# Delta rule: the transposes of three block-diagonal matrices on VectorE in 32x32 blocks, instead of on TensorE as products with the identity

## What is computed

```python
def gated_delta_chunked(q, k, v, log_a, beta, s0):
    ...
    a_mat = jnp.where(strict, jnp.einsum('bhncd,bhnsd->bhncs', kb, k) * decay_ij, 0.0)
    eye = jnp.eye(c, dtype=jnp.float32)
    t_inv = lax.linalg.triangular_solve(eye + a_mat, jnp.broadcast_to(eye, a_mat.shape),
                                        left_side=True, lower=True, unit_diagonal=True)
    u = t_inv @ (v * beta[..., None])
    w = t_inv @ (kb * jnp.exp(g)[..., None])
    ...
    def step(s, xs):
        ...
        v_new = u_i - jnp.einsum('bhcd,bhde->bhce', w_i, s)
        o_i = (jnp.einsum('bhcd,bhde->bhce', q_i * jnp.exp(g_i)[..., None], s)
               + jnp.einsum('bhcs,bhse->bhce', qk_i, v_new))
        ...
```

## Time and profile before

| | us |
|---|---|
| median of 3 runs | 2652.95 |
| lowest and highest | 2648.32, 2653.12 |
| the profiled execution, its own time | 2652.55 |
| its span in the trace | 2650.8 |

### The profile page before, as it was taken

The page is one execution under the profiler, slowest core; times in us unless marked ns, Lnnn a source line. Parts: engine busy times, 40 slices in busy tenths (PEclk is TensorE's granted clock), DMA queues, the critical chain, the costliest instruction groups (busy, mean ns, idle before and its releaser), DMA issues. The chain is left out here.

```text
span 2650.8 us, 42846 instructions
## 1 busy us (share of the span) xinstructions
PE 2271.0 (86%) x18263; PEld 1184.7 (45%) x18263; DVE 727.5 (27%) x1589; ACT 431.4 (16%) x886; POOL 311.1 (12%) x368
## 2 busy tenths in 40 slices
PE   6998899989888887887896998898988888888886
PEld 2456744454333343343443557755433334343332
DVE  3364545353011010111114454555210111111111
ACT  2323243210000000000001233341000000000000
POOL 0007200001111111110001006200111110000000
PEclk8999999989989898999998999999998999999998
DMA  7000098449999999999997110125899999999994
GB/s 319 32 16 35 6 347 329 157 162 356 426 423 416 416 418 405 418 420 418 383 392 309 41 46 19 68 70 228 345 426 420 416 419 423 416 410 415 417 418 187
DMA packets 96354, 781.08 MB, mean 295 GB/s; under 512 B 21736, under 2 KB 22136, under 8 KB 37280
## 3 DMA queue, kind: packets, MB, share of 16 engines
q1 hardware_dynamic: 74848, 740.46, 68.0%
q0 software_dynamic: 21312, 37.81, 3.8%
HBM read 772.55 MB, written 41.29 MB: 307 GB/s over the span
## 5 line engine op out<-in xcount | busy, mean ns | idle before, releaser
L1475 PE MATMUL banks<-arena,htreg 128*32 128x384 f32 (+2 forms) x5824 | 877.6, 533 | 208.0 <-DMA arena<-in_exp_w_gu 202.8
L1475 PEld LDWEIGHTS banks<-arena,htreg 128*32 128x32 f32 (+2 forms) x5824 | 403.4, 137 | 655.2 <-issue 508.2
L1500 PE MATMUL banks<-arena,modreg 128*32 128x512 f32 (+2 forms) x2184 | 403.9, 602 | 30.8 <-issue 27.2
L2236 DVE TENSOR_TENSOR modreg<-modreg,banks 128x384 f32<-128x384 f32 x74 | 41.0, 554 | 1040.9 <-ACT modreg L1792 1037.2
L1500 PEld LDWEIGHTS banks<-arena,modreg 128*32 128x32 f32 (+2 forms) x2184 | 137.8, 128 | 244.3 <-issue 241.5
L1042 PE MATMUL banks<-arena,htreg 128*128 128x512 f32 (+3 forms) x480 | 158.8, 490 | 0.0
L2391 DVE COPY modreg<-banks 128x512 f32<-128x512 f32 x68 | 47.0, 692 | 308.2 <-PE banks L1500 308.2
L1798 ACT ACTIVATE modreg<-banks 128x384 f32<-128x384 f32 x74 | 36.3, 490 | 531.2 <-PE banks L1491 531.2
L1792 ACT ACTIVATE modreg<-banks 128x384 f32<-128x384 f32 x74 | 36.3, 491 | 527.5 <-PE banks L1475 527.5
L2551 POOL DMA_INDIRECT y_d<-modreg,lst x68 | 67.5, 992 | 455.3 <-DVE modreg L2391 454.6
L1042 PEld LDWEIGHTS banks<-arena,htreg 128*128 128x128 f32 x480 | 89.6, 191 | 64.8 <-issue 60.9
(11 more groups left out here) (401 smaller groups left out, 2214.7 us busy)
## 6 DMA issues: line engine op xcount, KB each, us to landing
arena<-in_exp_w_gu SPq DMA_DIRECT2D x256, 1536.0 KB
arena<-in_exp_w_down SPq DMA_DIRECT2D x128, 1536.0 KB
arena<-in_w_mod SPq DMA_DIRECT2D x32, 1024.0 KB, 9.9
arena<-y_d SPq DMA_DIRECT2D x6, 3072.0 KB, 16.7
modreg<-in_w_mod SPq DMA_DIRECT2D x14, 1024.0 KB, 7.8
modreg<-mod_d SPq DMA_DIRECT2D x20, 512.0 KB
arena<-in_shared_w_gu SPq DMA_DIRECT2D x6, 1536.0 KB
arena<-in_w_in SPq DMA_DIRECT2D x4, 2048.0 KB, 13.0
```

The costliest lines, as they stand in the source:

```text
L1475: last = mm(gu_bank(n, half)[rows, 0:DE], src[:, k, rows], up4[q][:, i, DE * half:DE * (half + 1)], start=(k == 0), stop=(k == KD - 1))
L1500: last = mm(ps[4 + half][rows, :], actT[:, k, rows], dn3[q][:, k, 512 * half:512 * half + 512], start=(k == 0), stop=(k == KE - 1))
L2236: tt(act_, sgb, gu_bank(n, 1)[:, 0:DE], ALU.mult).then_inc(unit_act.sem, 1)
```

## The change

The product with `eye64` is gone from NT and from Pz32 and Pz64, and with it the copy of NT. In their place VectorE transposes in 32x32 blocks, from SBUF to SBUF: N into `W0[:, 1]`, and `PT` into `W0[:, 0]` (step P32) and `W1[:, 0]` (step P64). ScalarE copies only columns 256 to 511 of Pz32 and Pz64. p1 now carries the wait for the output addition of the block before, which NT had carried, because both write `D_.A`. pz waits for ScalarE's copy and for VectorE's P32 or P64.

```diff
@@ pe_order, dve_order
-                steps += [(b, s) for s in ("NT", "n2", "n4", "p1", "n8", "p2")]
+                steps += [(b, s) for s in ("n2", "n4", "p1", "n8", "p2")]
...
-            steps = [(-1, "S"), (0, "M"), (0, "N")]
+            steps = [(-1, "S"), (0, "M"), (0, "N"), (0, "NT")]
...
-                steps += [(b, "NT")] + [(b, "QK")] * o + [(b, s) for s in ("pt1", "pt2", "pt3", "pt32", "ks", "vx")]
+                steps += [(b, "QK")] * o + [(b, s) for s in ("pt1", "pt2", "pt3", "P32", "pt32", "P64", "ks", "vx")]
...
-                steps += [(b, "S")] + [(b, "o")] * o
+                steps += [(b, "S")] + [(b + 1, "NT")] * (b + 1 < NB) + [(b, "o")] * o
@@ TensorE
-                    for d, D_, pe_, act_d, dve_, pool_ in both:
-                        pe.wait_ge(dve_.sem, dve_.after(l, b, "N"))
-                        if b:
-                            pe.wait_ge(dve_.sem, dve_.after(l, b - 1, "o" if with_o(l, b - 1) else "vns"))
-                        pe_.done(blocks(D_.A, lambda r, g: D_.W0[r, 0, g, :], lambda r, g: eye64[r, :]), l, b, "NT")
...
                         pe.wait_ge(pool_.sem, pool_.after(l, b, "PT0"))
+                        if b:
+                            pe.wait_ge(dve_.sem, dve_.after(l, b - 1, "o" if with_o(l, b - 1) else "vns"))
                         pe_.done(blocks(D_.A, lambda r, g: D_.W1[r, 0, g, :], lambda r, g: D_.PT[r, g, :]), l, b, "p1")
...
-                            blocks(D_.C, lambda r, g: D_.PT[r, g, :], lambda r, g: eye64[r, :])
                             pe_.done(blocks(D_.C, lambda r, g: D_.B[r, B, g, :], lambda r, g: D_.PT[r, g, :], 256), l, b, "Pz" + w)
                         for d, D_, pe_, act_d, dve_, pool_ in both:
                             pe.wait_ge(act_d.sem, act_d.after(l, b, "Pz" + w))
+                            pe.wait_ge(dve_.sem, dve_.after(l, b, "P" + w))
@@ ScalarE
-                            act_d.done(fn(flat((D_.W0, D_.W1)[W]), D_.C, ACT.Copy), l, b, "Pz" + w)
+                            act_d.done(fn(flat((D_.W0, D_.W1)[W])[:, 256:512], D_.C[:, 256:512], ACT.Copy), l, b, "Pz" + w)
@@ VectorE
+                def front_t(b, d):
+                    _, D_, pe_, act_d, dve_, pool_ = both[d]
+                    dve.wait_ge(dve_.sem, dve_.after(l, b, "N"))
+                    dve_.done(dve.transpose(flat4(D_.W0[:, 1]), flat4(D_.W0[:, 0])), l, b, "NT")
+
+                def turned(b, W, w, was):
+                    for d, D_, pe_, act_d, dve_, pool_ in both:
+                        dve.wait_ge(dve_.sem, dve_.after(l, b, was))
+                        dve_.done(dve.transpose(flat4((D_.W0, D_.W1)[W][:, 0]), flat4(D_.PT)), l, b, "P" + w)
...
-                    for d, D_, pe_, act_d, dve_, pool_ in both:
-                        dve.wait_ge(pe_.sem, pe_.after(l, b, "NT"))
-                        dve_.done(dve.tensor_copy(D_.W0[:, 1], g64(D_.A)), l, b, "NT")
```

More of the change, by code:

```diff
@@ L2070, in front_n @@
                     dve_.done(tt(D_.W0[:, 0], D_.M[:, 0].rearrange("p (g j) -> p g j", g=HEADS), D_.mask[:, 0], ALU.mult), l, b, "N")
+                flat4 = lambda m: m.rearrange("p g j -> p (g j)")
+                def front_t(b, d):
[6 more added lines that the diff above has]
+                        dve_.done(dve.transpose(flat4((D_.W0, D_.W1)[W][:, 0]), flat4(D_.PT)), l, b, "P" + w)
                 for d, D_, pe_, act_d, dve_, pool_ in both:
@@ L2077, in _ @@
                     front_n(0, d)
+                for d in range(2):
+                    front_t(0, d)
                 for b in range(NB):
                     g64 = lambda m: m[:, 0:256].rearrange("p (g j) -> p g j", g=HEADS)
-                    for d, D_, pe_, act_d, dve_, pool_ in both:
-                        dve.wait_ge(pe_.sem, pe_.after(l, b, "NT"))
-                        dve_.done(dve.tensor_copy(D_.W0[:, 1], g64(D_.A)), l, b, "NT")
                     if with_o(l, b):
@@ L2091, in _ @@
                             dve_.done(tt(D_.PT, D_.PT, g64(D_.A), ALU.add), l, b, step)
+                    turned(b, 0, "32", "pt3")
                     for d, D_, pe_, act_d, dve_, pool_ in both:
@@ L2094, in _ @@
                         dve_.done(tt(D_.PT, D_.PT, g64(D_.A), ALU.subtract), l, b, "pt32")
+                    turned(b, 1, "64", "pt32")
                     for d, D_, pe_, act_d, dve_, pool_ in both:
@@ L2145, in _ @@
                         state(1)
+                        for d in range(2):
+                            front_t(b + 1, d)
                     else:
```

## The result

The changed kernel takes 2663.07 us (median of 17 runs, 2654.45 to 2678.53) where the kernel before takes 2653.28 beside it (17 runs, 2647.73 to 2670.71): a ratio of 1.0042, with a 95% interval of 1.0029 to 1.0055. That is slower by 9.8 us between the medians (about 11 by the ratio) where 4.5 us of gain were forecast, and outside the range. The profiled executions of the two kernels (2652.55 and 2663.07 us) lie close to their medians.

A forecast was written before the change was run, and what follows sets the result against it. TensorE was taken to bound the delta stages up to ks, VectorE from there to pt64. Gains of 3.5 (merges), 5.1 and 0.4 (boundaries) make 9.0, less 4.5 for the clock: 2652.55 - 4.5 = 2648.0 us, range 2645 to 2652.

The forecast's parts named there:

- What bounds the stage: Both delta stages: TensorE is the busy engine, 18.00 of 20.00 us; gains or losses move the expert stage one for one.
- The price of one transposition: One 256-column fp32 transposition on VectorE takes 0.42 us, and 0.33 where one follows another.
- dearer: Rival: each transposition takes 0.7 us, 5.3 us of the gain is eaten, time 2653; chance 0.12.
- waits for GpSimd: Rival: the transposition on VectorE waits until GpSimd's work ends, time 2659; chance 0.12.
- Merge 32 and merge 64: Merges in each block, counted from p3: pt32 at +3.02 instead of +3.81, ks at +4.50 instead of +5.22.
- 0.71 in five blocks, nothing in three: Merge gain at pt64: 0.71 us in five blocks, none where GpSimd holds vx; 3.5 us in all.
- The held three: Blocks 0 and 1 of layer 0 and 1 of layer 1: GpSimd delays vx, so no merge gain was counted.
- vx still ends 0.28 behind GpSimd: In the blocks where GpSimd delays VectorE, vx would come at +5.30 and still end at +6.69, pt64 staying at +9.02.
- the clock rival: Rival: no product runs at 1.2 GHz, time 2643.5, or 2641.5 if vx slips in ahead of GpSimd; chance 0.22.
- The boundaries: Between blocks, n2 comes 1.28 us earlier at four boundaries with an output; two without give 0.4 us together.
- What TensorE's pause does: Pauses ahead of Pz128 cost TensorE's clock: 1.1 us in each of four blocks, rounded to 4.5 us lost.
- A clock lost in every block: Both delta stages: the clock falls in all blocks; listed under mishaps of other kinds, together 0.06, without a size.

The follow-up runs named there:

- e4: Kernel after with only the boundary transposition of NT on VectorE, the merges left as before: 2649.11 us, ratio 0.9983 to the kernel before.
- e8: Kernel after with idle TensorE products ahead of Pz128 only in the three blocks where GpSimd holds VectorE, three batches per direction: 2655.09 us, ratio 1.0015.
- e3: Kernel before with VectorE's order altered, pt64 right behind ks and ahead of vx, nothing else: 2653.18 us, ratio 1.0001.
- e2: Kernel after with VectorE's order altered: ks, pt64, vx, qs, pt128, then qso and the state decay: 2642.18 us, ratio 0.9961 to the kernel before.
- e1: Kernel after with unread idle TensorE products between pz64 and Pz128 in all eight blocks: 2643.85 us, ratio 0.9964 to the kernel before.
- e5: Kernel before with four unread transpositions of a constant per block on VectorE ahead of ks, making pt64 late: 2672.86 us, ratio 1.0081.
- e7: Kernel after with GpSimd's decay inputs moved ahead of the decay output factors of the same block: 2657.53 us, ratio 1.0018 to the kernel before.
- e9: Kernel after with NT as a TensorE product again, so only the merges' transpositions are on VectorE: 2664.30 us, ratio 1.0045 to the kernel before.
- e6: e2 with one idle TensorE batch per direction behind the state product in the two blocks without an output: 2638.04 us, ratio 0.9945 to the kernel before.

## Why the prediction was wrong, step by step

- **What bounds the stage; that its gains move everything behind it.** Right. The experts' stage of layer 0 and the rest differ by 1.6 and 0.5 us. But what lies outside the two delta stages takes 2397 to 2414 us in the eleven profiled executions, so a few us of a stage's gain can't be found again in one span.
- **The price of one transposition: 0.42, and 0.33 where one follows another.** Right: 0.40 to 0.44, and 0.36 apart in the pair at 256.95. The rivals "dearer" and "waits for GpSimd" are both out by this one measurement. For the latter, the rule of the Trainium skill (SBUF — State Buffer, the shared port pair) draws the line correctly: the transposition, one input, was never stretched, and vx, 128x256 with two SBUF inputs, took 1.25 us instead of 0.41.
- **Merge 32 and merge 64.** Right within 0.1 us. p3 starts 0.73 ahead of pt3, as in the earlier trace rows, so at 255.41; P32 comes at +1.54 (+1.53 predicted), pt32 at +3.11 (+3.02), ks at +4.60 (+4.50).
- **0.71 in five blocks, nothing in three.** Nearly right: 4.2 us instead of 3.5. Block 2 of layer 0 gained 1.34: before, its pt64 had waited 0.47 us for pz64, and TensorE's shorter row took that away as well; of the other four, three gained 0.50 to 0.59 and one 0.80. The held three gained 0.15 each. "vx still ends 0.28 behind GpSimd" was wrong for the first vx and right for the second. The bonus of the clock rival, 2 us from vx slipping in ahead, did not come for that reason.
- **The boundaries: 1.28 four times, 0.2 twice.** Right: 1.31 and 0.17, which e4 shows without the rest. "At the two stage starts TensorE is cold either way; I count nothing" was wrong by 1.35 us in layer 1.
- **"What TensorE's pause does."** This is the step that failed. The sign and the mechanism were right, and the pauses are there: 1.97, 2.81 and 2.85 us in the held blocks (3.3 predicted), 1.48 to 1.94 in the others (1.7 predicted). The term was mis-sized, 4.5 us for what measured 16 to 18. Two factors of it are off. It should have struck "the three held blocks and about one of the other five": seven of eight were struck, and e8 shows that pauses of 1.5 to 2 us are enough. And I put down 1.1 us for each, arguing that ScalarE and VectorE alternate with TensorE behind the pause. But the stretch lasts beyond that, 6.8 to 10.2 us in five of the eight, and behind pt128 TensorE has kk, vn and the state product, which are on the chain as a whole: 2.3 us in block 1, and 2.7 in block 2 of layer 1, for vns alone, and up to 0.9 more between pt64 and pt128. Over the eight low stretches it is 2.0 to 2.3 us each. So both factors, the count and the price, were too small by about two, and 4.5 became 16 to 18.
- **Where I leaned on the wrong row.** The earlier trace rows show a clock of 1.00 with TensorE busy for 6.21 of 11.00 us, and I took it as evidence that pauses often cost nothing. It stands at a stage's end, and has 56 rows in 11 us, against 566 in 20 us within a stage: hardly any that could be slowed. It was luck, too: over the same piece of the stage's end, the profiled executions of the kernel after, e3, e4 and e8 have 0.84, each with a low stretch of 3.4 us. For the blocks, was the nearer row. "A clock lost in every block" was in my list, under mishaps of other kinds that share 0.06; the case deserved a price of its own. At the 2 to 2.7 us a block that the runs have since shown, 8 blocks less the 9.0 give 7 to 13 us slower, which takes in the result.
- **What I did not look for.** The pause ahead of Pz128 exists because VectorE does vx, qs, qso and the decay before pt64. I had read this ("from there VectorE is the bound") and used it only as a bound on the gain. e2 shows it as the thing to change: 21 us against the kernel after.

The Trainium skill describes a kernel that loses the clock over and over in waits between groups of products, and counts the loss as half of the low time (TensorE: Matmul & The Clock Gate, section HAM oscillation — how this bites in real kernels). By that, an estimate, the 51 us at low clock in the stages would cost 25.5 us. The runs here show 16 to 18. I take it that part of the low time lies under waits for VectorE and ScalarE; no run separates it.

What stays open: the two attention stages took 2.8 and 2.5 us more in the profiled execution after. In the other kernels the attention of layer 1 takes 64.6 (before, e1, e4, e5, e7, e9) or 66.9 to 67.1 us (after, e2, e3, e6, e8), with and without the transpositions, so I don't put it down to the change; what decides between the two values was not tried. Also open is what exactly makes the clock fall in a given block: block 2 of layer 0 kept it in the kernel after and lost it in e7 and e8 with the same steps on TensorE, and e4 lost it once behind 1.06 us.

## What to carry to other kernels

When work leaves TensorE, its time is not simply saved: look where TensorE will stand still, and price each such pause by the products that come behind it at half clock, not by its own length. Then put the vector step that TensorE waits for first in its engine's row; only together with that did the cheaper transposition pay (2638 to 2642 us, against 2663 without it and 2653 for either order before). Where a pause can't be closed, products that nothing reads can be worth more than they cost: 19 us here.

## What the runs showed of the hardware that I had not expected

- Pauses of 1.5 to 2.85 us in TensorE, one in each block of some 30 us, brought the granted clock from 0.98 to 0.91 and from 1.00 to 0.84 over the two stages, in stretches of 3.4 to 10.2 us. With idle products in the same pauses it was 0.98 and 1.00.
- A VectorE instruction with two SBUF inputs can get in between two of GpSimd's: vx took 0.46 us and GpSimd's product 1.24 instead of 1.04, while the next vx waited for that product to its end.
- A fp32 transposition in 32x32 blocks of 128x256 costs VectorE 0.40 to 0.44 us, as much as a plain instruction of that size, and loses nothing beside GpSimd (26 of the 48 in the kernel after overlap with one of its instructions).
